# Rebuilding the first block of a two-model transformer kernel: a split first norm, and attention woven into its projections

## The reference

```python
cond = silu(c)
mod = cond @ ada_w[i] + ada_b[i]                 # 1024 -> 6144: shift, scale, gate, twice
h = rmsnorm(x, norm1_g[i]) * (1 + sc1) + sh1
x = x + g1 * mixer(h)                            # what differs between the layers
h = rmsnorm(x, norm2_g[i]) * (1 + sc2) + sh2
x = x + g2 * ((silu(h @ w_gate) * (h @ w_up)) @ w_down)   # 2816 hidden columns
```

## Time and profile before

| | us |
|---|---|
| median of 3 runs | 1093.34 (1092.65 to 1093.69) |
| the profiled execution's own time | 1092.77 |
| its span | 1091.0 |
| PE busy | 1020.5 (94%) |
| DVE busy | 784.0 (72%) |
| ACT busy | 505.5 (46%) |
| POOL busy | 12.8 (1%) |

### The profile page before, as it was taken

One profiled execution on the slowest core, in us unless ns is written; L12 is line 12 of the kernel. 1 busy time (PEld: TensorE's weight loads), 2 busy tenths in 40 slices (PEclk: granted clock), 3 DMA queues, 4 the chain that ended last, 5 costly groups with the idle time before them and its releaser, 6 DMA issues.

```text
span 1091.0 us, 19815 instructions
## 1 busy us (share of the span) xinstructions
PE 1020.5 (94%) x7643; PEld 968.2 (89%) x7643; DVE 784.0 (72%) x1108; ACT 505.5 (46%) x773; POOL 12.8 (1%) x27
## 2 busy tenths in 40 slices
PE   4699889999999989999999999998998999999997
PEld 4696568999999988977899999998887989999997
DVE  5876884898769867675489876986774579876432
ACT  3435743544442354535454443234866553443433
POOL 3000000000000000000000000001000000000000
PEclk9996759999999979999999999997999889999998
DMA  9980458499748948263249974887502429974500
GB/s 303 353 305 4 154 195 268 143 362 317 273 166 318 342 150 319 78 232 117 78 139 362 316 274 163 318 318 255 190 1 77 157 79 355 359 248 157 200 29 39
DMA packets 144413, 232.18 MB, mean 213 GB/s; under 512 B 6249, under 2 KB 75409, under 8 KB 144353
## 3 DMA queue, kind: packets, MB, share of 16 engines
q1 hardware_dynamic: 142993, 228.75, 60.8%
q0 software_dynamic: 1072, 2.05, 0.8%
q10 hardware_dynamic: 288, 0.54, 0.2%
HBM read 230.27 MB, written 1.05 MB: 212 GB/s over the span
## 4 chain that ended last, share of the span: by engine, by line
PE 82%; DVE 7%; ACT 4%; issue 3%; DMA 2%; SPq 1%; DVEq 0%; ACTq 0%
PE M L1425 22%; PE M L1426 22%; PE M L1427 22%; PE AUX L1914 3%; PE AUX L1535 3%; DVE ACC L936 2%; DMA RAW<-in_ada_w 1%; DVE WL L913 1%; ACT WH L565 1%; DMA RAW<-in_wqkv_a 1%; PE AUX L1758 1%; PE AUX L1543 1%; PE M L1702 1%; DVE TMP L993 1%; PE M L1701 1%
## 5 line engine op out<-in xcount | busy, mean ns | idle before, releaser
L1425 PE MATMUL M<-XH,WH 128*128 128x256 f32 x1520 | 441.5, 290 | 13.1 <-DVE XL L998 11.9
L1426 PE MATMUL M<-XL,WH 128*128 128x256 f32 x1520 | 436.2, 287 | 0.0
L1427 PE MATMUL M<-XH,WL 128*128 128x256 f32 x1520 | 435.7, 287 | 0.0
L913 DVE TENSOR_TENSOR WL<-RAW,WH 128x2048 fp32r<-128x2048 f32 x136 | 308.4, 2286 | 84.1 <-ACT WH L565 84.0
L565 ACT ACTIVATE WH<-RAW 128x2048 fp32r<-128x2048 f32 x136 | 258.6, 1914 | 230.4 <-PE M L1427 155.9
L1425 PEld LDWEIGHTS M<-XH,WH 128*128 128x128 f32 x1520 | 298.3, 196 | 16.4 <-issue 14.6
L1426 PEld LDWEIGHTS M<-XL,WH 128*128 128x128 f32 x1520 | 298.3, 196 | 0.2
L1427 PEld LDWEIGHTS M<-XH,WL 128*128 128x128 f32 x1520 | 297.9, 196 | 0.0
L936 DVE SCALAR_TENSOR_TENSOR ACC<-ADA,COND,ACC 128x512 f32<-128x512 f32 x266 | 199.9, 751 | 9.7 <-DMA ADA<-in_ada_w 0.6
L1425 PE MATMUL M<-MH,WH 128*128 (+1 forms) x528 | 150.6, 285 | 0.6 <-DVE TMP L1013 0.6
L1427 PE MATMUL M<-MH,WL 128*128 (+1 forms) x528 | 149.4, 283 | 0.0
(11 more groups left out here) (236 smaller groups left out, 971.4 us busy)
## 6 DMA issues: line engine op xcount, KB each, us to landing
ADA<-in_ada_w SPq DMA_DIRECT2D x68, 1024.0 KB, 6.4
RAW<-in_w_gate SPq DMA_DIRECT2D x44, 512.0 KB, 6.7
RAW<-in_w_up SPq DMA_DIRECT2D x44, 512.0 KB, 7.7
RAW<-in_w_down SPq DMA_DIRECT2D x44, 512.0 KB, 6.1
RAW<-in_w_ffn_in SPq DMA_DIRECT2D x44, 512.0 KB, 6.1
RAW<-in_wqkv_b SPq DMA_DIRECT2D x24, 512.0 KB, 6.2
RAW<-in_w_ffn_out SPq DMA_DIRECT2D x22, 512.0 KB, 4.3
RAW<-in_w_in SPq DMA_DIRECT2D x16, 512.0 KB, 5.7
```

Of the source, the lines that this page charges most:

```text
L913: dve.tensor_tensor(WL[:, s, :], RAW[:, s, :], WH[:, s, :], ALU.subtract).then_inc(l_ready, 1)
L1425: pe.matmul(out_ap, wh, xh, start=start, stop=False, skip_group_check=True)
L1426: pe.matmul(out_ap, wh, xl, start=False, stop=False, skip_group_check=True)
L1427: return pe.matmul(out_ap, wl, xh, start=False, stop=stop, skip_group_check=True)
```

## The change

Eight edits, nearly all in the first layer.

1. **First norm in two halves.** Blocks are loaded in the order 0, 2, 1, 3 (shift and scale of tiles 0 to 3 first). DVE sums 4, 4, 8 and 4 of their rows; PE takes the rest straight from the loaded weights (`early_direct`). Two places take the place of four: block 1 waits for block 0's reduction, block 3 for block 2's. The squares of x move from ACT to DVE.
2. **Order of the queries.** Keys, values and both query unit halves for rows 0 to 3 first, then the reductions of blocks 1 and 3, then the rest.
3. **Attention starts among the last query products**: scores of pairs 0 and 1, the means and rotations of later tiles are spread between product tiles and over pairs 0 to 4.
4. **Softmax's division** moves into the transposes: POOL multiplies the identity by the reciprocals (four 128 x 128 instructions for each pair, `DG`), and PE multiplies by that diagonal matrix (a full float32 matmul) in place of a transpose; ACT's four scalings go.
5. **The two heads of a pair** alternate in the matmuls of `sa_scores` and `sa_rows`.
6. **Rows of the output projection** for its first four tiles (`out_rows`, 12 matmuls for each pair) are run within the attention, two pairs behind.
7. **Modulation blocks**: three rows for each pair (blocks 5 to 7), 8 and 9 after the attention, block 10 within the feed-forward stage, and its successor's load behind it in SPq.
8. **Norms 1 to 6** lose the means between product tiles; POOL adds the squares of tiles 0 to 3 (three 128 x 256 additions), and PE sums five groups after the unit, not eight.

```diff
+POSITIONS = [0, 2, 1, 3]
+EARLY_DVE = [4, 4, 8, 4]
+def attention_rows(b):
+    return [(5 + r // 8, r % 8) for r in range(3 * b, 3 * b + 3)]
 ...
+            def early_load(p, quarters=range(4)):          # SP
+                if p >= 2:
+                    sp.wait_ge(acc_red, p - 1)
 ...
+            def turners(b):                                # POOL
+                pool.wait_ge(sa_r, b + 1)
+                if b >= 2:
+                    pool.wait_ge(sa_tr, 2 * (b - 1))
+                for at in range(4):
+                    pool.tensor_scalar(DG[:, b % 2, at, :], IDENT, SM[:, b % 2, 5, at:at + 1], None, ALU.mult).then_inc(sa_pn, 1)
 ...
             for b in range(8):                             # DVE
+                if 1 <= b < 7:
+                    sa_max(b + 1)
+                if b + 4 < 9:
+                    qa_rope(b + 4)
+                    qa_add(b + 4)
+                for block_, kt in attention_rows(b):
+                    ada_sum(block_, 0, rows=[kt])
                 if b + 1 < 8:
                     sa_divide(b + 1)
 ...
+                if b in (0, 2, 4, 6):
+                    low(U0["wo_a"], b // 2)
+            ada_sum(8, 0)
+            ada_bias(7)
+            add_out("wo_a", 0, 0)
+            ada_sum(9, 0)
+            ada_bias(8)
             ada_bias(9)
-            ada_sum(10, 0)
-            add_out("wo_a", 0, 0)
 ...
                 low(base, 3)                               # DVE, feed_forward
+                if layer == 0:
+                    ada_sum(FOLDED, 0)
                 ada_sum(b0, int(b0 >= 24))
 ...
             for b in range(8):                             # PE
                 sa_turn(b)
+                if b < 2:
+                    qa_bank(4 + b, 0)
+                    qa_turn(4 + b)
+                if b >= 2:
+                    out_rows(b - 2)
+                if 2 <= b < 5:
+                    qa_bank(4 + b, 3)
+                    qa_turn(4 + b)
+                sa_rows(b, {0: 4, 3: 5, 6: 6}.get(b))
                 if b + 2 < 8:
                     sa_scores(b + 2)
 ...
-            def norm(n, done=0, blocks=()):                # PE
+            def norm(n):
+                for j in range(4, 6):
+                    mean_square(n, j)
+                pe.wait_ge(sq_sum, 3 * n)
+                token_means(AUX[:, 0, 0:2], SQS, ONES[:, 0:1], False, False)
+                for j in range(6, KT):
+                    mean_square(n, j)
```

More of the change, by code:

```diff
@@ new lines, in keys_and_values @@
+            def keys_and_values(kts, first, last):
+                for kt in kts:
+                    pe.wait_ge(xin_ready, kt + 1)
+                    for e in range(2):
+                        cols = slice(kt * 256 + e * P, kt * 256 + e * P + P)
+                        mm = three(AUX[:, 2 + e, :], WH[:, 0, cols], WL[:, 0, cols], *operand(kt), first and kt == kts[0] and e == 0,
+                                   last and kt == kts[-1])
+                if last:
+                    mm.then_inc(w_used, 1)
@@ new lines, in queries @@
+            def queries(k, tau0, half, n, first):
+                s = slot(base, k)
+                if n == 0:
+                    pe.wait_ge(l_ready, base + k + 1)
+                for q in range(4):
+                    xh, xl = operand(4 * half + q)
+                    cols = slice(q * 512 + n * P, q * 512 + n * P + P)
+                    mm = three(M[:, tau0 + n, :], WH[:, s, cols], WL[:, s, cols], xh, xl,
+                               first and q == 0 and n % 2 == 0, not first and q == 3)
+                if n == 3:
+                    mm.then_inc(w_used, 1)
+                elif not first and n == 1:
+                    mm.then_inc(qa_prod, 1)
@@ L1739, in _ @@
                 if b + 2 < 8:
                     sa_scores(b + 2)
-                if b % 2 == 0 and b > 0:
-                    ada_reduce(5 + b // 2)
-                sa_rows(b)
-            ada_reduce(9)
-            group(U0["wo_a"], 0, 0, 0, 1)
-            group(U0["wo_a"], 1, 1, between=early_means(1))
+            out_rows(6)
+            pe.wait_ge(vc_ready, ROW_TILES)
+            ada_reduce(7)
+            out_rows(7)
+            base = U0["wo_a"]
+            taus = [(4 + n, n * P) for n in range(4)]
@@ L1980, in _ @@
             unit(base, 2, 0, sets[0], range(0, 4), operand, False, True)
-            unit(base, 3, 0, sets[1], range(0, 4), operand, False, True, between=early_means(5))
+            unit(base, 3, 0, sets[1], range(0, 4), operand, False, True)
             feed_forward(2)
-            norm(6, 4)
+            norm(6)
             for m in range(2):
```

617 lines of the change are left out of this document (393 added, 224 removed).

## The result

| | before | after |
|---|---|---|
| median of the runs | 1093.51 us (4 runs, lowest 1092.65) | 1106.86 us (1104.12 to 1107.52, 4 runs) |
| ratio | | 1.0099, 95% interval 1.0074 to 1.0125 |
| the profiled execution: own time, span | 1092.77, 1091.0 | 1106.79, 1105.0 |
| POOL busy | 12.8 | 57.2 |
| DVE busy | 784.0 | 780.4 |

A forecast was written before the change was run, and what follows sets the result against it. PE, busy 94% of the span, was taken as the bound, with loads and DVE bounding the start. -6.8 + 11.2 - 10.5 = -6.1 took 1092.8 to 1086.7, with 0.6 for the median 1087 us; range 1079 to 1095, whole 1067 to 1104.

The forecast's parts named there:

- The start and the first products: Up to the attention: first product at 41.3 us in place of 45.5, first turned weights near 95 in place of 100.6.
- The loop over pairs: Attention loop: DVE's work 48.2 us plus some 10 of named waits, lasting 58 and ending at 151.5 us.
- a period of the pairs over 9 us: Attention loop: a sign listed beforehand that would show the forecast wrong.
- Rotations 4, 6 and 8 wait 1.5 to 2.5 each: Attention loop: these rotations wait 1.5 to 2.5 us each for a turn on PE behind `sa_turn` and `out_rows`.
- 0.35 us: Attention loop: assumed time of each POOL instruction that scales the identity; no profile row showed it.
- 1.3 and 2.6: Attention loop: us for a pair's six transposes as full float32 matmuls on PE, at the full and the lower clock.
- rival (b): Attention loop: PE's clock stays low, as at 0.64 before; loop 8 us longer, 1095 us; chance 0.20 together with Rival (d).
- Rival (c): Attention loop: diagonal matrices late, chain 4.8 + 4p (p per POOL instruction) against DVE's 7.2; 1103 or 1106 us; chance 0.18.
- Rival (d): First block: attention isn't overlapped and the block ends as before, 1094 us; chance 0.20 together with rival (b).
- After the loop: From the loop's end to the feed-forward stage's first product: 151.5 to 184.5 us, in place of 191.3, 6.8 gained so far.
- Block 10: Feed-forward stage: first products 33 us after its start, PE stands 8.8 us; 11.2 lost in sum, bounds 6 and 13.
- Norms 2 to 6: Fewer groups of squares: 1.3 us gained at norms 3, 5 and 6, 3.3 at 2 and 4; sum 10.5, bounds 6 and 14.

The follow-up runs named there:

- The reordering alone: Changed kernel with PE's rotations of the next query tile moved ahead of the pair's turned weights, or of the output-projection rows: 1097.00 us, ratio 1.0019 to before.
- the kernel with everything that helped: Changed kernel plus rotations ahead, gate/up units ahead of block 11, gate/up loads 0 and 1 earlier, diagonals on DVE: 1083.66 us (on POOL 1084.38).

## Why the prediction was wrong

**The start and the first products: right.** First product forecast at 41.3, profiled at 39.5; first turned weights forecast near 95, profiled at 93.3. That both came some 1.8 us sooner than forecast is in part luck: in other executions of kernels with the same start they stood at 42.2 to 43.0 and 97 to 99 (see the last section).

**The loop over pairs: the step that failed.** "The loop lasts 58 and ends at 151.5" was 73.1, ending at 166.4 (74.8 from the first reciprocal, where the forecast's 58 begin): 15 of the 20 us by which the span missed its forecast. The sum of DVE's work was nearly right, 48.2 against 45.8 busy from the first reciprocal to the loop's end. The low parts waited 1.31 us in two of the four cases, where 1.4 was put down for all. The prediction's own sign of being wrong, a period of the pairs over 9 us, was there (9.2 to 12.7). Three sizes were wrong:
- "Rotations 4, 6 and 8 wait 1.5 to 2.5 each", 4.5 to 7.5 us, of which the sum of 58 took the low end (5.6 + 4.5 is its "some 10"). They waited 5.79, 4.28 and 4.32, and rotation 7, whose wait was put at nothing, 4.74: 19.1 us. I priced the wait as what PE has to do ahead of the rotation (`sa_turn`, `out_rows`), and forgot that `sa_turn` itself waits for POOL, and POOL for DVE's reciprocal just done. The wait is the whole way round. The reordering alone, with all the work left in, shortens the loop from 73.1 to 64.8.
- "0.35 us" for POOL's instruction: 0.58 us each, 4.14 instead of 2.35 for the four where a low part runs beside them. With the diagonals on DVE the loop goes on from 64.8 to 59.7 and 59.3, so the order and the diagonals together account for nearly all of the 15 us.
- "1.3 and 2.6" for a pair's turned weights at the two clocks: the forecast went by 1.3, and left the rest to rival (b). They took 2.6 to 3.1 in six pairs of eight. This lies inside the same 15 us.

Rival (c) had the direction and, by chance, the price (1103 to 1106), but its condition was wrong as well. It set the chain of 4.8 + 4p against DVE's 7.2 as if the two ran side by side; at p = 0.58 that gives 7.1, no loss. (The terms that it lists add up to 4.0 to 4.6, not 4.8, so at p = 0.58 the chain would be 6.3 to 6.9.) In truth a part of DVE's 7.2, the rotation and the three rows, lay inside the chain, and so did the projection's row. That the four follow a reciprocal, where DVE "next reads PSUM", kept POOL nearly free in six pairs of eight (2.34 to 2.65), as said; in the other two the low part came next.

Rival (b), the low clock, came in part: the loop's granted clock was 0.78, above the 0.64 before. PE was slow where it had stood for POOL (2.93 us for its twelve records behind stops of 4.08 and 4.48), so I read it as a part of the circle. That is argued from the trace; no run changes the clock alone. Rival (d) is out: projection rows do run in the pairs, and taking them out costs 0.7%.

**After the loop: right but for 2.6 us.** 33 us forecast, 35.6 measured to the first gate/up product; the waits for loads were 1.50 + 3.96 + 0.68, about 4 forecast, and PE's reduction and the bias of block 9 took 2.2 where 1.1 was put down.

**Block 10: right.** The first products came 34.0 us after the stage's start (33 forecast), PE stood for 8.05 us of it (8.8). The stage with norm 2 became 8.8 us longer, where 11.2 less 3.3 were forecast. What I didn't see is that most of the price was one of order: with the two low parts ahead of block 11 the stop falls from 8.05 to 1.9 us, and the way from norm 1's root to norm 2's is 204.4 us, against 213.5 in the changed kernel. With block 10 out of the stage it was 201.4, so some 3 us of its price are left.

**Norms 2 to 6: mechanism right, size off.** 10.5 forecast; 7.5 in the profile with edit 8 alone. Norms 2 and 4 gave 3.2 and 3.0 (3.3 each forecast), norm 6 gave 1.6 (1.3 forecast). Norms 3 and 5 gave nothing: the sum had no POOL addition beside a low part in them (only its bound of 6 had them late), and DVE's low parts took 5.53 and 5.03 instead of 4.48.

## What to carry to other kernels

When work is put between two steps of a loop, follow the loop once all the way round through the queues, and add up what stands in the circle; comparing "the chain" with "the engine's work" takes them as parallel when one queue holds both. A small operation that the next step of a busy engine needs belongs ahead, in its queue, of anything that waits for a slower engine. Before an operation is given to an idle engine, ask what stands behind it in that engine's queue: ACT made the same matrices in half of POOL's time and gained nothing, until one instruction behind them was moved. And a shorter stage isn't yet a shorter kernel: 5 us less in the pairs were under 1 us in the kernel with everything that helped.

## What the runs showed of the hardware that I had not expected

- POOL's scaled 128x128 identity takes 0.58 us (2.34 for four), on ACT 1.28 for four, on DVE 0.87 for four. A POOL add of 128x256 takes 0.74 where nothing runs beside it.
- POOL and a DVE instruction with two SBUF inputs hold each other up, in both directions: POOL's four took 1.8 us longer beside a low part of 2.3; DVE's two low parts took 1.05 us longer beside two POOL additions, which took 5.33 in place of 1.6.
- The same code started in two ways. In five of the twelve profiled executions with the changed start the 128x1 groups of the first norm's squares speed up under way (16 records in 1.84 to 2.3 us) and the first product comes at 39.2 to 39.7. In the other seven they take 3.41, the first product comes at 42.2 to 43.0, and the first turned weights come some 5 us later (92 to 93 against 97 to 99). The granted clock is no guide to the first of these stretches: from 10 to 20 us it reads 1.00 in all twelve, and in the seven up to 40 us, while the records go at 0.22 us each. In the five it reads 0.50 from 30 to 40 us, which the records there bear out. Times of two kernels within 5 us of each other are therefore compared here by medians, and stretches within one profile by their length. How much of the spread among a kernel's executions comes from this isn't shown, as each kernel has one profile.
